# Loading and turning a block's small parameters after the token tiles instead of among them

## The reference

```
h    = rms_norm(x, norm_mix)
proj = h @ w_in                      # 1024 -> 10760 columns, split in 16 parts
...                                  # HGRN2, mLSTM, short convolution, Conformer convolution (width 31)
merged = sum_b sigmoid(gates_b) * (branch_b @ w_branch_b)
x    = x + merged @ w_out
x    = x + square(relu(rms_norm(x, norm_mlp) @ w_up)) @ w_down
y    = rms_norm(x, norm_final)
```

## Time and profile before

| | us |
|---|---|
| runs | 2221.77, 2223.40, 2223.69 |
| median | 2223.4 |
| the profiled execution | 2223.99 |
| its span in the trace | 2222.2 |
| TensorE busy, of this span | 2194.8 (99%) |
| VectorE, GpSimd, ScalarE busy | 1108.7, 1103.9, 652.9 |

### The profile page before, as it was taken

How to read it: one execution, slowest core, us unless ns; L and a number is a source line. 1 busy time by engine, 2 the same in 40 slices (tenths; PEclk the granted TensorE clock), 3 DMA queues, 4 the chain that set the end, 5 groups by cost and what they waited for, 6 DMA issues and landing times. The chain is left out here.

```text
span 2222.2 us, 33414 instructions
## 1 busy us (share of the span) xinstructions
PE 2194.8 (99%) x13524; PEld 2078.7 (94%) x13524; DVE 1108.7 (50%) x1733; ACT 652.9 (29%) x1145; POOL 1103.9 (50%) x1367
## 2 busy tenths in 40 slices
PE   7999999999999999999999999999999999999998
PEld 6999999999999999999999999889989899898897
DVE  7522221799754445534441465555464453653625
ACT  5344442333321111232222122133232232232332
POOL 4644444677343233222225664517485674754751
PEclk9999999999999999999999999999999999999999
DMA  4333332112222202112333554301211102102022
GB/s 136 118 98 100 117 93 68 48 49 68 54 87 60 59 21 59 50 59 86 83 119 120 186 181 159 116 10 49 76 29 48 58 19 77 55 22 77 20 67 81
DMA packets 172669, 171.20 MB, mean 77 GB/s; under 512 B 6690, under 2 KB 147318, under 8 KB 172507
## 3 DMA queue, kind: packets, MB, share of 16 engines
q1 hardware_dynamic: 169885, 159.03, 23.4%
q0 software_dynamic: 2304, 8.91, 1.1%
q10 hardware_dynamic: 326, 1.12, 0.1%
HBM read 135.07 MB, written 34.33 MB: 76 GB/s over the span
## 5 line engine op out<-in xcount | busy, mean ns | idle before, releaser
L972 PE MATMUL acc<-h_hi,w_hi 128*128 128x368 f32 (+2 forms) x2080 | 684.5, 329 | 4.1 <-ACT staging L1541 2.0
L974 PE MATMUL acc<-h_hi,w_lo 128*128 128x368 f32 (+2 forms) x2080 | 677.8, 326 | 0.0
L973 PE MATMUL acc<-h_lo,w_hi 128*128 128x368 f32 (+2 forms) x2080 | 677.1, 326 | 0.0
L1947 POOL TENSOR_TENSOR w_lo<-w_raw,w_hi 128x256 fp32r<-128x256 f32 x512 | 384.1, 781 | 479.5 <-ACT w_hi L1470 479.5
L972 PEld LDWEIGHTS acc<-h_hi,w_hi 128*128 128x128 f32 x2080 | 391.8, 188 | 9.9 <-issue 6.3
L973 PEld LDWEIGHTS acc<-h_lo,w_hi 128*128 128x128 f32 x2080 | 392.1, 188 | 0.2
L974 PEld LDWEIGHTS acc<-h_hi,w_lo 128*128 128x128 f32 x2080 | 391.6, 188 | 0.0
L1470 ACT ACTIVATE w_hi<-w_raw 128x1024 fp32r<-128x1024 f32 (+1 forms) x147 | 140.7, 959 | 358.2 <-PE acc L974 183.5
L2312 DVE TENSOR_TENSOR x<-pz,x 128x512 f32<-128x512 f32 x214 | 144.3, 688 | 91.0 <-PE pz L974 88.4
L1947 POOL TENSOR_TENSOR a_op<-a_raw,a_op 128x256 fp32r<-128x256 f32 x196 | 155.8, 834 | 27.1 <-ACT a_op L1470 13.6
L2312 DVE TENSOR_TENSOR a_raw<-acc,a_raw 128x368 f32<-128x368 f32 (+1 forms) x112 | 44.7, 420 | 205.6 <-ACT a_raw L1833 118.7
(11 more groups left out here) (526 smaller groups left out, 4635.4 us busy)
## 6 DMA issues: line engine op xcount, KB each, us to landing
w_raw<-in_w_in SPq DMA_DIRECT2D x72, 512.0 KB, 4.5
w_raw<-in_w_up SPq DMA_DIRECT2D x32, 512.0 KB, 4.3
gate_values<-staging SPq DMA_DIRECT2D x28, 544.0 KB, 3.2
gsig<-gate_values SPq DMA_DIRECT2D x28, 544.0 KB, 3.7
w_raw<-in_w_down SPq DMA_DIRECT2D x18, 512.0 KB, 3.6
b_raw<-branch_outputs POOLq DMA_DIRECT2D x16, 544.0 KB, 5.7
w_raw<-in_w_branch SPq DMA_DIRECT2D x16, 512.0 KB, 4.9
f_raw<-in_w_down SPq DMA_DIRECT2D x14, 512.0 KB, 5.6
```

The lines of the kernel that those rows point to most:

```text
L972: pe.matmul(out, lh, rh, start=first, stop=False, skip_group_check=more)
L973: pe.matmul(out, lh, rl, start=False, stop=False, skip_group_check=more)
L974: return pe.matmul(out, ll, rh, start=False, stop=last, skip_group_check=more)
L1947: return pool.tensor_tensor(out, x, y, op)
```

## The change

```diff
@@ sync
             for i in range(NT + 1):
                 sp.dma_start(xin[0:rows_of[i], i, :], x_tiles[i]).then_inc(x_in[i], 16)
-                if i == 0:
+                if i == 1:
                     sp.dma_start(ident, a["con"][:, C_ID:C_ID + P]).then_inc(con_in, 16)
-                if i == 1:
-                    load_params(sp, PARAMS[3:])
-                    sp.dma_start(nrow[0:8, :], a["norm_mix"][0].rearrange("(a b) -> a b", b=P)).then_inc(params_in, 16)
-                    sp.dma_start(nrow[8:16, :], a["norm_mlp"][0].rearrange("(a b) -> a b", b=P)).then_inc(params_in, 16)
                 if i in (3, 5):
                     unit_load(i // 2 - 1)
+            load_params(sp, PARAMS)
+            sp.dma_start(nrow[0:8, :], a["norm_mix"][0].rearrange("(a b) -> a b", b=P)).then_inc(params_in, 16)
+            sp.dma_start(nrow[8:16, :], a["norm_mlp"][0].rearrange("(a b) -> a b", b=P)).then_inc(params_in, 16)
@@ tensor
             for i in range(NT - 3):
                 turn_tokens(i)
-                if i == 0:
-                    turn_params()
+            turn_params()
@@ scalar
             act.dma_start(gain_r[:, :], a["norm_mix"]).then_inc(sem("gain_in"), 16)
-            load_params(act, PARAMS[:3])
@@ vector
-                if i == 2:
+                if i == NT - 2:
                     params_out()
```

## The result

The changed kernel takes 2225.16 us (median of 22 runs, 2222.31 to 2228.79), the kernel before 2222.4 us (22 runs beside them, 2221.09 to 2224.8). The ratio is 1.0012, 95% interval 1.0006 to 1.0017: **slower by 2.7 us**, inside the predicted range, but on the other side of the forecast of -0.3. The profiled execution took 2226.11 us, its span is 2224.3.

A forecast was written before the change was run, and what follows sets the result against it. TensorE was taken as the bound, busy 2194.8 of 2222.2 us, so only idle time could move. The later arm, max(-1.3, -0.3) = -0.3 us, took the median from 2223.4 to 2223.1 us; range 2221.3 to 2226.4.

The forecast's parts named there:

- the forecast of -0.3: Whole kernel: the later of the tokens' arm and the parameters' arm decides, -0.3 us; chance 0.62 within about 1 us.
- the parameters' arm: VectorE's split of tile 3, held by the parameters' landing: L - 22.5, taken as -0.3 us, bounds -1.2 and +3.2.
- L: Time when the tenth parameter is in, ending TensorE's wait before the parameter transposes; taken as 22.2 us.
- the sum: Work of one DMA engine on token tiles plus parameters, taken as the same in either order, ending at 22.2 us.
- The tokens' arm: VectorE's split of tile 3, held by the tokens' chain and the turning at i = 6: 0.74 - d, -1.3 us.
- The gain d: Time the tokens gain when transfers leave the queues ahead of their tiles: taken as 2.0 us, bounds 0 and 2.59.
- The first term: In the tokens' arm, the split of tile 3 starts 0.74 us later for the parameters' turning and copy.
- One for one: A microsecond on VectorE's split of tile 3 is a microsecond of the whole, later as well as earlier.
- The early removal, the identity, ScalarE's issues: Removing `params_out` at i = 2 and ScalarE's three early issues, and issuing the identity some 0.5 us later: priced at nothing.
- the parameters are late: Rival: TensorE waits behind tile 4 for the small loads until L = 25.7, +3.2 us, 2226.6 us; chance 0.18.
- One after another: Rival: small loads follow the tiles singly, each at a fixed price, at most 1.26 us: +12.3 us; chance 0.05.

The follow-up runs named there:

- s4: The changed kernel with the parameters turned two tiles later, behind tile 6, and VectorE's copies at i = 8: 2221.39 us against 2223.09 for the kernel before.
- s11: The changed kernel with fourteen extra identity transposes on TensorE ahead of its wait for the parameters: 2225.03 us against 2222.23 for the kernel before.
- s12: The changed kernel with the parameters turned behind tile 6, timed again on another chip: 2221.25 us against 2222.23 for the kernel before.
- s10: The changed kernel with the load of `conv_conformer_w` behind the other nine parameters: 2224.18 us against 2222.23 for the kernel before.
- s3: The kernel before with only the turning moved (TensorE's behind tile 4, VectorE's to i = 6), loads unchanged: 2224.8 us against 2223.09.
- s1: The changed kernel with the 31 rows of `conv_conformer_w` loaded as two transfers, 16 and 15 rows: 2223.26 us against 2223.09 for the kernel before.
- s8: The changed kernel itself, timed once more: 2224.97 us against 2221.9 for the kernel before.
- s9: The kernel before, loads unchanged, with the parameters turned behind tile 6 and copied out in step 8: 2221.82 us against 2221.9.
- s7: The changed kernel with the 31 rows of `conv_conformer_w` loaded twice and all eleven loads waited for: 2227.63 us against 2221.9 for the kernel before.
- s2: The changed kernel with `conv_conformer_w` alone back at the head of ScalarE's queue: 2225.02 us against 2223.09 for the kernel before.
- s6: The changed kernel with nine more one-row loads ahead of the ten, all nineteen waited for: 2225.85 us against 2221.9 for the kernel before.

## Why the prediction was wrong

**The step that failed is the parameters' arm, at "on an engine that never pauses the sum of both is the same whatever the order, so L = 22.2".** L was 24.79 and 24.02 in two executions. The form of the arm was right: L + 0.90 + 0.52 = 26.21 is to the hundredth what the trace shows. With 24.8 instead of 22.2 the arm gives +2.3 and not -0.3.

What the sum had right is the work of the one engine: the wide load's own increment, which was the last before the nine narrow ones, came at 23.11 and 22.34 in two executions of the changed kernel and at 21.65 to 22.57 in s4, s11 and s12, whose loads are the same, 22.3 on average. What it left out, without a reason, is what comes behind: nine loads whose increments arrive 0.18 us apart, 1.64 us in all, when no other parameter behind them covers them. The landing of the last tile, 22.2, was taken as the end of the sum. In the kernel before nobody waited for such a tail: there the ten had all arrived by 10.45, and TensorE turned them at 12.61. The order does matter: s10, with the wide load last, ends at 23.13, though its engine moved the same rows. The remaining 0.8 us of the 24.79 is the late wide load of that execution, and why it was late is open.

**The tokens' arm.** The gain d was taken as 2.0; the scaling of tile 5 shows 2.5, near the bound of 2.59. The first term was 0.74 and s3 shows 1.5, of which 0.49 may be chance of that execution. That makes -1.0 instead of -1.3, and s1, where TensorE waits only 0.21 us for the parameters, shows -1.13 at the split. It didn't matter, since the other arm decided by over 3 us.

**One for one.** Right: 2.30 us at the split of tile 3 are 2.31 at GpSimd's `w_lo`, and the whole stage's 2.82 are 2.83 at the wait behind 50 us. What was missing is the stretch behind the wait, 0.5 us longer in the profiled execution and 0.1 in s8. A wait of TensorE was priced at its length, and the products behind it ran slower as well.

**The early removal, the identity, ScalarE's issues.** Priced at nothing, and nothing is to be seen of them: TensorE's first transpose (at 9.61) waits for VectorE's scaling and not for the identity, and s9, with step 2 emptied, is level with before.

**The rivals.** The case that came true is "the parameters are late", given 0.18 and priced at +3.2 us for L = 25.7; it was +2.7. That it came near is in part luck: it had the last issue at 16.9 and 8.8 us to its landing, where the trace has 14.79 and 10.0, and it had no tail of increments. "One after another" is out at its prices, a fixed 1.26 us each or 0.47; at 0.18 us each it is what happened behind the wide load. The size of all this lies within 0.2%, as said; the sign was the wrong one.

## What to carry to other kernels

A small transfer is not cheap because it is small: ask over how many DMA engines its rows divide, and whether a larger load that is waited for anyway can go behind it. When loads are moved back behind others, their consumers have to be moved behind the landing too, with the landing read from a trace. Here the same late loads lose 2.7 us with the turning behind tile 4, and behind tile 6 they lose nothing: the medians are 1 to 1.7 us below the kernel before, a gain that the intervals don't yet show.

## What the runs showed of the hardware that was not expected

- 62 KB in 31 rows of 2 KB go over one DMA engine of sixteen: alone on it a row takes 0.08 us and the whole 2.49 us (s7, 25 GB/s). As 16 + 15 rows they no longer leave one engine working at the end, with one transfer more.
- Loads of one row to eight at the end of the queue: their rows start at most 0.09 us apart, their increments arrive 0.18 us apart (s2, s6, s7, s8 and the changed kernel), so nine of them let the last one arrive 1.4 us behind the last row. With the wide load behind them the last increment is 0.40 us behind the last row (s10).
- The landing of the last parameter varied by 0.8 us between two executions of the same kernel, and between 23.30 and 24.75 over five executions with the same ten loads (the changed kernel, s8, s4, s11, s12). Whether the times scatter more for it is not shown: the changed kernel's runs spread over 6.5 us against 3.7, but s8's over 3.1 against 4.2.
